# FFN activations of a two-block transformer kernel in tiles that start at 0 modulo 256 bytes instead of 64

## The reference, cut to what matters

```python
def swiglu(u, w_gate_up, w_down):            # called f in the kernel, 22 blocks of 128 hidden columns
    gate, up = jnp.split(u @ w_gate_up, 2, axis=-1)
    return (jax.nn.silu(gate) * up) @ w_down

def sqrelu_mlp(x, w1, w2):                   # called m and n in the kernel, 32 blocks each
    h = jax.nn.relu(x @ w1)
    return (h * h) @ w2
...
h = h + swiglu(rmsnorm(h, ffn_norm[l]), w_gate_up[l], w_down[l])
...
h = h + sqrelu_mlp(rms_norm(h, norm_gain[layer, 1]), mlp_w1[layer], mlp_w2[layer])
```

## Time and profile before

| what | value |
|---|---|
| median of the runs shown | 2085.68 us (fastest 2085.51, one of the three at 4145.21) |
| time of the profiled execution | 2085.78 us |
| its span in the profile | 2084.0 us |
| TensorE busy | 2066.3 us (99%) |
| VectorE, ScalarE, GpSimd busy | 1521.2, 986.7, 719.2 us |
| stage f (from its first to its last matmul) | about 471 to 813 us |
| stage m | about 1072 to 1409 us |
| stage n | about 1734 to 2071 us |

### The profile page before, as it was taken

One profiled execution on the slowest core, in us unless ns is written; L12 is line 12 of the kernel. 1 busy time (PEld: TensorE's weight loads), 2 busy tenths in 40 slices (PEclk: granted clock), 3 DMA queues, 4 the chain that ended last, 5 costly groups with the idle time before them and its releaser, 6 DMA issues.

```text
span 2084.0 us, 31976 instructions
## 1 busy us (share of the span) xinstructions
PE 2066.3 (99%) x12566; PEld 1746.9 (84%) x12566; DVE 1521.2 (73%) x2061; ACT 986.7 (47%) x1655; POOL 719.2 (35%) x588
## 2 busy tenths in 40 slices
PE   9999999999999999999999999999999999999998
PEld 6888688888999998877789898988975678899997
DVE  6866775658988886388768777776578757877774
ACT  4433564445444444356554343444537755334344
POOL 2301520027443334065463232311147746333321
PEclk9999999999999999999999999999999999999999
DMA  6333135223333433211133323233520012333321
GB/s 182 91 105 88 52 101 172 72 66 98 104 98 102 122 92 101 81 51 55 37 91 111 112 90 113 92 111 99 145 77 2 1 53 86 106 108 95 110 93 51
DMA packets 293303, 188.44 MB, mean 90 GB/s; under 512 B 9249, under 2 KB 287009, under 8 KB 293153
## 3 DMA queue, kind: packets, MB, share of 16 engines
q1 hardware_dynamic: 292864, 186.18, 29.9%
q10 hardware_dynamic: 288, 0.21, 0.0%
HBM read 183.48 MB, written 2.10 MB: 89 GB/s over the span
## 4 chain that ended last, share of the span: by engine, by line
PE 94%; DVE 3%; ACT 1%; issue 1%; DMA 0%; POOL 0%; ACTq 0%; SPq 0%; DVEq 0%
PE ps L544 92%; PE ps L578 2%; DVE wl L517 1%; ACT wh L507 1%; DVE sb_small L3481 0%; DMA p_xt<-in_x 0%; DVE ns_x L3527 0%; DVE ns_x L3526 0%; DVE H L681 0%; DVE nt_pts L3509 0%; ACT XH L565 0%; ACT xb_x L565 0%; DVE tp_up L2317 0%; DVE tp_up L2330 0%; DVE XL L573 0%
## 5 line engine op out<-in xcount | busy, mean ns | idle before, releaser
L517 DVE TENSOR_TENSOR wl<-raw,wh 128x1024 fp32r<-128x1024 f32 (+1 forms) x334 | 429.2, 1299 | 231.7 <-ACT wh L507 231.1
L544 PE MATMUL ps<-xb_x,wh 128*128 128x256 f32 (+1 forms) x1584 | 388.6, 336 | 1.5 <-DVE st_k L2783 0.6
L507 ACT CAST wh<-raw 128x1024 fp32r<-128x1024 f32 (+1 forms) x334 | 322.0, 980 | 129.7 <-PE ps L544 118.1
L544 PEld LDWEIGHTS ps<-xb_x,wh 128*128 128x128 f32 x1584 | 267.2, 189 | 30.0 <-DVE H L681 0.9
L544 PE MATMUL ps<-tt_t,wh 128*128 128x256 f32 x1536 | 272.5, 279 | 0.9 <-ACT tp_q L2259 0.5
L544 PE MATMUL ps<-xb_x,wl 128*128 128x256 f32 (+1 forms) x792 | 265.0, 335 | 0.0
L544 PEld LDWEIGHTS ps<-tt_t,wh 128*128 128x128 f32 x1536 | 235.9, 188 | 4.8 <-ACT tp_q L2259 1.2
L544 PE MATMUL ps<-XH,wh 128*128 128x512 f32 (+1 forms) x616 | 227.2, 369 | 1.2 <-DVE H L711 0.8
L544 PE MATMUL ps<-XH,wl 128*128 128x512 f32 (+1 forms) x616 | 222.2, 361 | 0.0
L544 PE MATMUL ps<-XL,wh 128*128 128x512 f32 (+1 forms) x616 | 222.0, 360 | 0.0
L544 PE MATMUL ps<-tt_t,wl 128*128 128x256 f32 x768 | 213.1, 277 | 0.0
(11 more groups left out here) (442 smaller groups left out, 4553.2 us busy)
## 6 DMA issues: line engine op xcount, KB each, us to landing
raw<-in_mlp_w SPq DMA_DIRECT2D x128, 512.0 KB, 4.0
raw<-in_w_gate_up SPq DMA_DIRECT2D x44, 512.0 KB, 3.8
raw<-in_w_in SPq DMA_DIRECT2D x28, 512.0 KB, 3.7
raw<-in_sb_w_qkv SPq DMA_DIRECT2D x24, 512.0 KB, 3.6
raw<-in_w_down SPq DMA_DIRECT2D x22, 512.0 KB, 5.9
raw<-in_w_out_mix SPq DMA_DIRECT2D x16, 512.0 KB, 3.6
raw<-in_w_kv SPq DMA_DIRECT2D x16, 512.0 KB, 3.8
raw<-in_nsa_w_kv SPq DMA_DIRECT2D x12, 512.0 KB, 3.7
```

The costliest lines, as they stand in the source:

```text
L507: e.copy(shaped(WH[i % NH], i), source(i)).then_inc(*w_hi.up(i))
L517: e.tensor_tensor(shaped(WL[i % NH], i), source(i), shaped(WH[i % NH], i).bitcast(F), ALU.subtract).then_inc(*w_lo.up(i))
L544: return e.matmul(out, a, b, start=start, stop=stop, skip_group_check=True)
```

## The change

Two new pairs are made. XF lies 64 bytes ahead of XB over the same memory and starts at byte 127232; XN lies 192 bytes behind the start of X and starts at byte 77568. Both are 0 modulo 256, and so are their second tiles. Stages f and m read and write XF where they used XB, stage n uses XN where it used X. To make room for the last 192 bytes of XN, the small tile `sb_small` (256 bytes, used by the sparse attention before stage n) moves from behind `nrms` to a place right behind X; `rs`, `acc`, `sq`, `tmp` and `nrms` move by 256 bytes and keep their remainder, and everything from PH0 on stays where it was. All other stages keep XB and X.

The lists of instructions of the two programs are the same on all five engines, with the same semaphores and values; only names and addresses differ. So nothing is moved in the order of work.

```diff
@@ -241,16 +241,18 @@
     XAT = base[0]
     X = Pair(sb("XH", [128, 8, S], R), sb("XL", [128, 8, S], R))
+    sb_small = sb("sb_small", [128, 64])
     RS0 = base[0]
...
     nrms = sb("nrms", [128, 80])
-    sb_small = sb("sb_small", [128, 64])
     base[0] += 192
     PH0 = base[0]
     XB = Pair(*(Phase(PH0 + 4 * 8 * S * i, f"xb{i}").sb("x", [128, 8, S], R) for i in range(2)))
+    XF = Pair(*(Phase(PH0 - 64 + 4 * 8 * S * i, f"xf{i}").sb("x", [128, 8, S], R) for i in range(2)))
+    XN = Pair(*(Phase(XAT + 192 + 4 * 8 * S * i, f"xn{i}").sb("x", [128, 8, S], R) for i in range(2)))
...
-                act_hi(e, XB, "ff", o - 1, H[:, o - 1, :], col("ffn_norm", o - 1))
+                act_hi(e, XF, "ff", o - 1, H[:, o - 1, :], col("ffn_norm", o - 1))
...
-            dve_lo(e, XB, "ff", o, H[:, o, :], col("ffn_norm", o))
+            dve_lo(e, XF, "ff", o, H[:, o, :], col("ffn_norm", o))
...
-                act_hi(e, XB, "m", o - 1, H[:, o - 1, :], col("ng", 8 + o - 1))
+                act_hi(e, XF, "m", o - 1, H[:, o - 1, :], col("ng", 8 + o - 1))
...
-    ff = Ffn("f", GU, "ff", XB, XAT, "xa", [(v_made, ("xq", 7))])
-    fm = Ffn("m", [4] * 8, "m", XB, XAT, "st", [(g_made, ("fe", 7))])
-    fn = Ffn("n", [4] * 8, "n", X, PH0, "ns", [(v_made, ("nq", 7))])
+    ff = Ffn("f", GU, "ff", XF, XAT, "xa", [(v_made, ("xq", 7))])
+    fm = Ffn("m", [4] * 8, "m", XF, XAT, "st", [(g_made, ("fe", 7))])
+    fn = Ffn("n", [4] * 8, "n", XN, PH0, "ns", [(v_made, ("nq", 7))])
...
-                act_hi(e, X, "n", o - 1, H[:, o - 1, :], col("ng", 24 + o - 1))
+                act_hi(e, XN, "n", o - 1, H[:, o - 1, :], col("ng", 24 + o - 1))
```

More of the change, by code:

```diff
@@ L1932, in act_xattn @@
         e.wait_ge(*h_new.at("xa", 7))
-        act_hi(e, XB, "ff", 7, H[:, 7, :], col("ffn_norm", 7))
+        act_hi(e, XF, "ff", 7, H[:, 7, :], col("ffn_norm", 7))
         act_square(e, "ff", 7, H[:, 7, :])
@@ L2720, in act_stick @@
         e.wait_ge(*h_new.at("st", 7))
-        act_hi(e, XB, "m", 7, H[:, 7, :], col("ng", 15))
+        act_hi(e, XF, "m", 7, H[:, 7, :], col("ng", 15))
         act_square(e, "m", 7, H[:, 7, :])
@@ L2838, in low @@
             e.wait_ge(*h_new.at("st", o))
-            dve_lo(e, XB, "m", o, H[:, o, :], col("ng", 8 + o))
+            dve_lo(e, XF, "m", o, H[:, o, :], col("ng", 8 + o))
         for o in range(8):
@@ L3437, in act_nsa @@
         e.wait_ge(*h_new.at("ns", 7))
-        act_hi(e, X, "n", 7, H[:, 7, :], col("ng", 31))
+        act_hi(e, XN, "n", 7, H[:, 7, :], col("ng", 31))
         act_square(e, "n", 7, H[:, 7, :])
@@ L3659, in low @@
             e.wait_ge(*h_new.at("ns", o))
-            dve_lo(e, X, "n", o, H[:, o, :], col("ng", 24 + o))
+            dve_lo(e, XN, "n", o, H[:, o, :], col("ng", 24 + o))
         for o in range(8):
```

## The result

The changed kernel takes 2088.79 us (median of 22 executions, 2088.38 to 2089.28) against 2085.53 for the kernel before (median of 22, one of them the 4145.21 us of the table above). The ratio is 1.0016, with a 95% interval of 1.001 to 1.0022: slower by 3.3 us, where 11.5 us less were forecast. The time lies outside the range.

What follows compares the result with a forecast made beforehand. The prediction took TensorE to bound f, m and n; gains of 10.1 us (256 columns) and 1.4 us (512 columns), 11.5 in all, took 2085.7 to 2074.2 us, with an 8-in-10 range of 2071.8 to 2078.5.

Steps and rivals of the forecast that it cites:

- What bounds the kernel: In f, m and n TensorE sets the time, busy 99% of the span, so shorter matmuls come off the total.
- Does the start address matter: Matmuls of 256 columns starting at 0 instead of 64 modulo 256 take 113.3 ns, not 120.0: 6.7 ns less each.
- Part 1: 1728 matmuls of 256 columns in the pair jobs now read from 0: 10.1 us gained over f, m and n.
- The early stretch of f: Before 553.55 us in f, 102 affected matmuls lie in stretches set by VectorE and ScalarE and gain nothing.
- VectorE's cover: In later halves of f VectorE finishes 0.42 us before TensorE needs its result; 0.2 us of gain booked as lost.
- Part 2: 288 matmuls of 512 columns in each stage's first four jobs now read from 0: 1.4 us gained.
- Part 3: Everything else, such as ScalarE and VectorE writes and the moved small tiles, costs nothing; 3.4 us at the very most.
- The one on the slower side: Rival: TT is quick because its remainder differs from its surroundings; with XF at 0 it loses 15.4 us, 2101.1; chance 0.02.
- The rule weighed: The skill's matmul gap, 109 ns for 256 columns, ignores start address, so time stays 2085.7 us; the prediction held it undecisive.

Runs made afterwards that it cites:

- the streams: Kernels without the computation that run float32r matmuls alone on TensorE, no other engine beside them; a copied pair job took 9.83 us, no kernel time compared.
- the kernel with TT split: The changed kernel with TT's fourth block, p4's operand, in a pair of its own at 64 modulo 256; 2078.61 us, ratio 0.9968 to the kernel before.

## Why the prediction was wrong

**What bounds the kernel: right.** TensorE in f, m and n set the time, and what its pace added there reached the total: 3.4 us by starts, 3.3 by medians.

**Does the start address matter: half right, and this is the step that failed.** The prediction took the 6.7 ns between "120.0 ns each" and "113.3 ns each" for the price of a start at 64 against one at 0. The row was read rightly, but it held three things at once: TT's address, the weights' address, and the 24 XB matmuls in front. The quick pace belongs to the sequence. By the streams 256 columns have 120.0 at 64, 117.8 at 0, and 113.3 at 0 only when something such as XB at 64 has just run. The change took away the very thing that made TT quick: behind XF at 0, TT has 117.7 ns in the later pair jobs. That the start at 0 alone is worth 2.2 ns and not 6.7 stood in the trace of before: p4, TT after `fm_h`, has 118 ns. The prediction took "past the first three of TT" from a product that followed XB and looked neither at the three left out (121, 122, 116: the shift itself) nor at p4, and the mean of 277 ns in the earlier trace rows hid that a quarter of TT was slower.

**Part 1, 10.1 us gained: wrong in size and sign.** In one pair job of m, 36 XB matmuls fell from 120.0 to 117.7 (0.08 us less), 36 TT matmuls rose from 113.3 to 117.7 (0.16 more), 12 stayed, and the slower or quicker first matmuls at each switch are gone (some 0.01 less). That gives 0.07 more, and 9.82 became 9.89. Over f, m and n the pair jobs got 0.84, 0.32 and 0.98 us longer; m's first two, which hold the late starts and run at the quick pace up to 1113 us, got 0.50 shorter. The early stretch of f, which the prediction gave to VectorE and ScalarE, lost nothing: the first three groups of gate and up jobs took 21.26, 20.16 and 20.10 us and take 20.77, 20.12 and 20.05, while each of the seven later ones is 0.20 longer. The price of VectorE's cover was not tried by this change, since TensorE got slower; in the kernel with TT split, the matmuls of each of those seven get 0.38 us shorter than before the change, and the chain of waits there is still TensorE alone after 566.91 us, so VectorE follows.

**Part 2, 1.4 us gained: wrong sign.** The split of 120 and 227 ns into 107 or 214 by columns and a constant of 13 had the constant follow the address alike at both sizes. That the constant was 13 at both sizes at 64 was no finding: the 107 was the difference of the two paces, so the rest comes out the same by the way it was worked out. And the address doesn't act alike at both: going from 64 to 0 takes 2.2 ns from 256 columns and adds 6.6 to 512. 288 matmuls at 6.6 ns are 1.9 us, and 1.65 were measured. The lower bound of this gain was set at 0, with no row that excluded a loss, so the range had no room for one.

**Part 3: right.** With n back on X, n is as before although the small tiles have moved.

**The rivals.** None had the whole mechanism. The one on the slower side, that the remainders must differ, had the direction (TT slows, XF gains nothing) and got 0.02, and TT's rise from 277 to 281 ns is the sign that the prediction had named for it. Its closing condition, that the previous product's tile matters to more than the first matmul, is what the streams found, for 256 columns at 0. The reason given against it, that 21 TT matmuls in a row keep 113.3 ns with no XB between, was none, since the quick pace, once set, holds for 72 matmuls and more in the streams. Its price of 15.4 us was too high, for it took 6.7 ns from all 48 TT matmuls, where 36 lose 4.4, and gave XF nothing back.

**The rule weighed.** The trace has 113.3, 117.8 and 120.0 ns for the same 256 columns between weight loads. The Trainium skill, "TensorE: Matmul & The Clock Gate", section "Back-to-back issue gap", gives an isolated matmul N/2.4 + 2.5 ns, 109 for 256 columns, and names no address. No run here shows an isolated matmul; for matmuls with a weight load before each the trace doesn't agree with one number for a size. The answer that the prediction drew from it, no effect, was nearer to the result than the forecast, but the runs refute its reason.

**What stays open.** Why the pace depends on the distance between the two operands, and what it is that an insert or a late start shifts, is not shown. Whether reads of the moving operand and weight loads get in each other's way in the memory was not tested: no run separates the two. That other places than -64 also have more than one pace was seen but not followed up, the 229 and 233 ns of 512 columns at +64 in the kernel with weights at 0 among them. Open too is why the first pair job of n in the kernel after stays at 117.7 when that of m, also behind 512 columns at 0, ran at 113.3. The steps just ahead differ, though: 233, 233 and 234 ns by turns in m, 231 and 236 in n. In the streams, 256 columns at 0 are quick behind 512 at 0 with steps of 233, 233 and 234, as in m. This again looks like a place in a cycle.

## What to carry to other kernels

Before a difference between two groups is called a property of their operands, look at all the places where the same operand stands, behind different predecessors: one TT product behind another neighbour would have turned this forecast. Where a kernel is bound by float32r matmuls with weight loads between them, starts are a free setting worth a few per cent of a matmul: 512 columns want the weights' remainder modulo 256, 256 columns the one 64 bytes below it together with a product at the weights' remainder just ahead. It is to be measured on streams of matmuls alone, in the order of the kernel, with what runs ahead of them, and then in the kernel, since the same matmul ahead worked in one place and not in another. An unknown cost gets a bound on both sides even when it seems to follow from a neighbouring size.

## What the runs showed of the hardware that was not expected

- The pace of float32r matmuls with a weight load before each depends on where the moving operand starts relative to the weights, modulo 256 bytes: behind 512 columns at the weights' remainder 116.7 to 120.0 ns at 256 columns, 173.3 to 176.7 at 384, 226.7 to 234.3 at 512, all at a granted clock of 1.00, the 2.4 GHz level. The weights' own remainder is the best place for 512 columns (226.7) and among the worst for 256 (120.0).
- 256 columns at a distance of -64 have two steady paces, 117.8 and 113.3 ns (384 columns: 176.7 and 173.3). Which one is set by the few matmuls before, and holds for all 72 or 84 matmuls of a stream that runs without a late start; steps of 391 and 390 ns ended it, one of 241 ns didn't. Smaller splits were seen at other distances (120.0 and 118.7 ns, 117.8 and 116.7). One extra matmul of 384 columns ahead of each 84 was worth 6.9 us of 2089.
- Streams of TensorE alone gave the time of a pair job in three arrangements, 9.83, 9.90 and 10.07 us against 9.83, 9.89 and 10.07 in the kernels, though in these VectorE, ScalarE and transfers use the same memory all the while.
